# Softmax maxima of ordinary heads brought into the queries' row by two small DMAs instead of two identity matmuls and a PSUM copy

## What is computed

```python
s = jnp.einsum('bqhd,bkhd->bhqk', qb, kb).astype(jnp.float32) * scale + bias[None]
s = jnp.where(valid[None, None, None, :], s, MASK_VALUE)
p = jax.nn.softmax(s, axis=-1)
return jnp.einsum('bhqk,bkhd->bqhd', p.astype(vb.dtype), vb)
```

## Time and profile before

| what | value |
|---|---|
| median of 3 runs | 1634.67 us (1633.82 to 1635.09) |
| profiled execution, its own time | 1639.75 us |
| its span, first to last instruction | 1638.0 us |
| TensorE matmuls busy | 1580.3 us, 96% |
| VectorE, ScalarE, GpSimd busy | 1037.9, 826.2, 662.9 us |
| mean granted clock of TensorE | 0.988 |

### The profile page before, as it was taken

One profiled execution on the slowest core, in us unless ns is written; L12 is line 12 of the kernel. 1 busy time (PEld: TensorE's weight loads), 2 busy tenths in 40 slices (PEclk: granted clock), 3 DMA queues, 4 the chain that ended last, 5 costly groups with the idle time before them and its releaser, 6 DMA issues.

```text
span 1638.0 us, 42689 instructions
## 1 busy us (share of the span) xinstructions
PE 1580.3 (96%) x17344; PEld 1181.3 (72%) x17344; DVE 1037.9 (63%) x2134; ACT 826.2 (50%) x1541; POOL 662.9 (40%) x667
## 2 busy tenths in 40 slices
PE   7999999999999999999988999999999999999976
PEld 3455455458677777767767888899888899888853
DVE  7977867747565576556435666666666666666654
ACT  6655545522121111111125777767777777677763
POOL 2543433311101121111313655655655665656653
PEclk9999999999999999999998999999999999999978
DMA  6656566473524524542777877877777877778663
GB/s 245 218 193 219 188 212 221 181 258 147 207 75 169 206 96 150 181 167 79 222 220 185 208 196 199 198 187 192 171 193 196 201 192 184 172 190 197 158 170 84
DMA packets 306459, 299.99 MB, mean 183 GB/s; under 512 B 179384, under 2 KB 239816, under 8 KB 304216
## 3 DMA queue, kind: packets, MB, share of 16 engines
q1 hardware_dynamic: 305736, 296.60, 61.8%
q0 software_dynamic: 528, 0.66, 0.2%
HBM read 150.87 MB, written 83.54 MB: 143 GB/s over the span
## 4 chain that ended last, share of the span: by engine, by line
PE 68%; DMA 4%; POOL 2%; ACT 2%; SPq 2%; DVE 1%; issue 1%; DVEq 0%; ACTq 0%; POOLq 0%
PE bank L1154 10%; PE bank L2007 8%; PE bank L1130 6%; PE bank L1133 6%; PE bank L1132 6%; PE bank L1740 5%; PE bank L1742 5%; PE bank L1743 5%; DMA stages<-rows 4%; PE bank L1930 3%; PE bank L2061 2%; PE bank L2063 2%; PE bank L2062 2%; PE bank L2027 2%; PE bank L1933 2%
## 5 line engine op out<-in xcount | busy, mean ns | idle before, releaser
L1740 PE MATMUL bank<-middle,weights 128*128 128x128 f16 x1792 | 311.2, 220 | 2.3 <-ACT middle L1756 1.3
L1742 PE MATMUL bank<-middle,weights 128*128 128x128 f16 x1792 | 310.9, 220 | 0.0
L1743 PE MATMUL bank<-middle,weights 128*128 128x128 f16 x1792 | 310.8, 220 | 0.0
L2383 POOL TENSOR_TENSOR rows<-rows 128x640 f16<-128x640 f32 (+4 forms) x128 | 172.8, 1350 | 274.6 <-ACT rows L2184 274.6
L1130 PE MATMUL bank<-middle 128*128 128x256 f16 x784 | 213.7, 273 | 0.5 <-DVE stages L1270 0.5
L1133 PE MATMUL bank<-middle 128*128 128x256 f16 x784 | 213.7, 273 | 0.0
L1132 PE MATMUL bank<-middle 128*128 128x256 f16 x784 | 213.7, 273 | 0.0
L2007 PE MATMUL bank<-entry,stages 128*128 128x512 f16 x768 | 190.6, 386 | 5.3 <-DVE stages L2250 5.3
L1740 PEld LDWEIGHTS bank<-middle,weights 128*128 128x128 f16 x1792 | 176.0, 98 | 3.7 <-issue 2.8
L1742 PEld LDWEIGHTS bank<-middle,weights 128*128 128x128 f16 x1792 | 176.0, 98 | 0.4
L1743 PEld LDWEIGHTS bank<-middle,weights 128*128 128x128 f16 x1792 | 175.8, 98 | 0.0
(11 more groups left out here) (169 smaller groups left out, 3956.0 us busy)
## 6 DMA issues: line engine op xcount, KB each, us to landing
entry<-in_x SPq DMA_DIRECT2D x64, 512.0 KB, 3.8
h_ops<-middle SPq DMA_DIRECT2D x16, 1792.0 KB, 6.1
middle<-h_ops SPq DMA_DIRECT2D x112, 256.0 KB, 5.4
middle<-h_ops SPq DMA_DIRECT2D x49, 512.0 KB, 8.0
residual<-entry SPq DMA_DIRECT2D x32, 512.0 KB, 3.0
middle<-middle SPq DMA_DIRECT2D x128, 128.0 KB, 3.2
out<-entry SPq DMA_DIRECT2D x31, 512.0 KB, 2.9
entry<-residual SPq DMA_DIRECT2D x30, 512.0 KB, 5.6
```

Of the source, the lines that this page charges most:

```text
L1740: nc.tensor.matmul(dst, wh, hop3[:, o, 0, kt, :], start=(kt == 0 and s < 2 and pair == 0), stop=False, skip_group_check=True)
L1742: nc.tensor.matmul(dst, wh, hop3[:, o, 1, kt, :], start=False, stop=False, skip_group_check=True)
L1743: mm = nc.tensor.matmul(dst, wl, hop3[:, o, 0, kt, :], start=False, stop=(kt == 3), skip_group_check=True)
L2383: nc.gpsimd.tensor_tensor(r16[:, j, 1, c:640], r32[:, j, c:640], r16[:, j, 0, c:640], ALU.subtract).then_inc(A["rpl_done"], 1)
```

## The change

The identity matmuls, their semaphore `mrow_mm` and the copy from PSUM are gone. ScalarE, in the same place of its order, waits for the maxima and issues two DMAs from its own queue, each of which copies one float16 from each of 128 partitions of `m16` into 128 neighbouring places of partition 64 of `qm`. Each adds 16 to `mrow_done`, so what waited for a row now waits for 32. A wait for the scores of the same head in the tile before is added, since these read the row that is written over. The branch transposes no longer wait for rows; they wait for the bank's last reader in every round.

```diff
-        def max_rows(pe, t, h):
-            pe.wait_ge(A["max_done"], 2 * (HEADS * t + h + 1))
-            if t > 0 or h > 0:
-                pe.wait_ge(A["mrow_done"], HALF * t + h // 2)
-            for back in (h - 3, h - 2):
-                if back >= 0 and round_at(t, back):
-                    of, r = round_at(t, back)
-                    pe.wait_ge(A["ytl_done"], 2 * of + r + 1)
-            for j in range(2):
-                mm = nc.tensor.matmul(tra[:, j * P:(j + 1) * P], m16[:, h // 2 % 2, j:j + 1].to_broadcast([P, P]),
-                                      ident16[:, :], start=True, stop=True)
-            mm.then_inc(A["mrow_mm"], 1)
...
             if j == 0:
-                at_least(dve, A["mrow_mm"], HALF * t + h // 2 - 1)
+                at_least(dve, A["mrow_done"], 32 * (HALF * t + h // 2 - 1))
...
         def first_maxima(pe, x):
-            if x == 2:
-                max_rows(pe, 0, 0)
...
                 if k == 0:
-                    pe.wait_ge(A["mrow_done"], HALF * t + h // 2 + 1)
+                    pe.wait_ge(A["mrow_done"], 32 * (HALF * t + h // 2 + 1))
...
-            def branch_transposes(t, r, rows):
+            def branch_transposes(t, r):
...
-                pe.wait_ge(A["mrow_done"], rows)
-                if t == LAST and r > 0:
-                    pe.wait_ge(A["ytl_done"], 2 * t + r)
+                at_least(pe, A["ytl_done"], 2 * t + r)
...
-                    if t1 < ATILES:
-                        max_rows(pe, t1, h1)
...
             def max_row(t, h):
...
-                act.wait_ge(A["mrow_mm"], HALF * t + h // 2 + 1)
-                nc.scalar.activation(queries(qm, slice(DH, DH + 1), h, slice(0, AT)), tra[DH:DH + 1, 0:AT],
-                                     ACT.Copy).then_inc(A["mrow_done"], 1)
+                act.wait_ge(A["max_done"], 2 * (HEADS * t + h + 1))
+                if t > 0:
+                    act.wait_ge(A["st_mm"], seq(t - 1, h, len(groups(t - 1))))
+                for j in range(2):
+                    row = queries(qm, slice(DH, DH + 1), h, slice(j * P, (j + 1) * P))
+                    nc.scalar.dma_start(row, m16[:, h // 2 % 2, j:j + 1]).then_inc(A["mrow_done"], 16)
```

More of the change, by code:

```diff
@@ L1563, in build @@
             bias_k_loaded mask_done fg_loaded wob_hi wob_lo out_mm out_done
-            rows_set shift_done rexp_done rph_done rpl_done max_mm max_done mrow_mm mrow_done st_mm bias_done exp_done ph_done pl_done
+            rows_set shift_done rexp_done rph_done rpl_done max_mm max_done mrow_done st_mm bias_done exp_done ph_done pl_done
             pv_mm rc_done ya_done yt_mm yth_done ytl_done ss_done ms_done rstd_done fin_done""".split()
@@ L2090, in last_head @@
                 values(LAST, HEADS - 2)
-                branch_transposes(LAST, 1, HALF * ATILES)
+                branch_transposes(LAST, 1)
                 values(LAST, HEADS - 1)
@@ L2094, in last_head @@
                     output(LAST, i, 6, 9)
-                branch_transposes(LAST, 2, HALF * ATILES)
+                branch_transposes(LAST, 2)
                 for i in range(2, 4):
@@ L2126, in head @@
                     of, r = round_at(t, h)
-                    branch_transposes(of, r, min(HALF * t + (h + 1) // 2 + 1, HALF * ATILES))
+                    branch_transposes(of, r)
                 other(t, h, 2)
```

## The result

The changed kernel takes 1743.18 us (median of 4 runs, 1738.38 to 1748.16) against 1634.88 us before (4 runs); the ratio is 1.0663 with a 95% interval of 1.063 to 1.0697. It is 6.6% slower, 108 us. The profiled execution has a span of 1746.4 us against 1638.0.

A forecast was written before the change was run, and what follows sets the result against it. TensorE was taken to bound the attention part, 890 to 1550 us. Terms -6.1 - 0.2 + 1.0 = -5.3 us took 1634.67 to 1629.4 us, 0.32% faster; range 1626.5 to 1647 us, the forecast's own 1627 to 1632.

The forecast's parts named there:

- The bound: Attention part, 890 to 1550 us: TensorE busy 657.2 of 660 us, so only less TensorE work gains time.
- the rooms for L: Time from ScalarE's possible issue to the row's need, four places per tile: 4.16, 6.27, 4.45 and 4.49 us.
- the third place: Third ordinary head of a tile: 4.45 us from ScalarE's possible issue until the first score matmul needs the row.
- the 1.26 us: ScalarE's two DMA issues per row: 0.60 us each with 0.06 between, claimed to cost nothing.
- (c): ScalarE is held longer by its DMA issues, deciding from about 1.3 us per issue; 1650 us; chance 0.06.
- TensorE's 6 us: Saturated attention stretch: removing the identity matmuls of 55 rows at 0.11 us takes 6.1 us off the path.
- With one issue ahead, L is 0.06 + 0.66 + 2.6 = 3.3 us: Time from ScalarE's possible issue to the second DMA's landing, priced by 64 KB copies; no wait in tiles 2 to 14.
- my upper bound of 6.2: Longest expected time from ScalarE's possible issue to landing: 0.06 + 0.66 + 5.5 us, from a copy behind other traffic.
- Rival (a): Row lands late for the score matmuls, deciding from 4.5 us; 1658 us at 5.0, 1707 at 6.2; chance 0.22.
- the early rows: Two rows at the attention part's start with room of 2.98 and 2.56 us; TensorE stands 1.0 us together.
- Rival (b): Small DMAs stretch the transposing DMAs from 5.0 to 6.17 us, delaying ScalarE and GpSimd; 1651 us; chance 0.07.
- 256 pieces are few beside their own traffic: Argument that the row's pieces per pair would not slow transposing DMAs, which land in 5.0 us at 0.77 load.

The follow-up runs named there:

- the version with blocks: The changed kernel, with VectorE first transposing the maxima in 32 x 32 blocks, so each row DMA carries 4 pieces of 64 bytes; 1631.06 us, repeated 1632.49 us.
- the idle kernel: The kernel before, plus the change's two column-to-row DMAs per ordinary head into a spare row that no score waits for; 1718.61 us against 1634.33.

## Why the prediction was wrong

**What was right.** The bound: TensorE was saturated, and the rooms for L were the right thing to compute, though in the third place ScalarE issues as soon as the maximum is there and does not wait for its activation, so that room was 0.4 us longer than I had it (in the trace before, the maximum is there at 1246.19, and I counted from 1246.61). ScalarE's two issues took more than the 1.26 us that I had counted (1.87 us in the place shown and in the median), which is 0.9 us each, under the 1.3 us where (c) decides: behind them ScalarE stood for the next row maximum (L2160 waited 72.4 us for L1957 from 1000 to 1500 us). Of TensorE's 6 us the version with blocks gains 3.3 and 2.3 us by the medians. The rest is about the noise of such a comparison, and its cause is not shown; the transposes took 5.4 us in that kernel in place of 5.0.

**The step that failed** is "With one issue ahead, L is 0.06 + 0.66 + 2.6 = 3.3 us", with the price of a 64 KB copy for a DMA of 128 pieces of 2 bytes. The small DMAs of 1000 to 1500 us took 6.3 us each in the median, so L was about 0.5 + 6.3 = 6.8 us, as the pairs of the trace have it too, outside my upper bound of 6.2. (The 5.5 in that bound is of L1870, a copy of 128 KB and not of 64.) The sentence "for which no row has a price" named the hole, and I then filled it with the row nearest in size. The row was nearest in bytes and not in what counts: the issues of the 64 KB copies have 64 pieces of 1 KB, and they go to 64 partitions. With 4 pieces of 64 bytes L was 3.7 us, near the 3.3 of the sum: the term that was mis-sized is the price of the pieces.

**Rival (a)** is what happened to the scores, with L = 6.8: TensorE's matmuls waited 93 us for L2011 in a kernel that is 108 us longer. The lower clock adds at most 26 us and 6 us are saved, so these terms give 87 to 113 us. The formula of (a) gives at this L 2.64 + 0.53 + 2.35 + 2.31 = 7.8 us per tile, 102 us in 13 tiles, and with 8 for the early rows 1738 us. The waits measured are 93 / 16 = 5.8 us per tile, and the sum had no term for the clock, so it is in part luck that 1738 lies so near to 1743. I had put 0.22 on it, and its price at 6.2, 1707 us, lay outside my range.

**Rival (b)** happened as well: transposes at 8.3 us, where I had costed 6.2. "256 pieces are few beside their own traffic" misled: as packets they are few (0.6% of the engines), as completions they are not. Alone, with no score waiting, it is worth 84 us. The two don't add: 84 for (b) alone, 108 for both, and 31 us between the two kernels if TensorE's 7 us are counted; a TensorE that stands for a row gives ScalarE and GpSimd the time that they lost to the transposes. This is argued; the sign for it is that TensorE's weight loads waited 49.7 us for GpSimd in the idle kernel and 11.9 us in the changed one. Of the 31 us up to 23 can be the clock (mean 0.974, against 0.987 in the idle kernel).

**What the small writes do** is shown in size but not in mechanism. Shown: with 2-byte pieces it counts whether they go to one partition or to 128 (84 against 9 us with as many packets); 16 pieces of 16 bytes for the same bytes in one partition cost 5 us; neighbouring 2-byte places cost more than places 8 bytes apart (84 against 36 us); some 10 ns of delay of the transposes per write; and the other DMAs are held up, SyncE's copies too (2.6 to 3.9 us). That each such write reads, changes and writes back a few bytes and that these wait for each other would fit it. A rival that no run separates is that several DMA engines take turns at the one partition, whatever they write; the spread writes (36 us) speak against it as the whole, not as a part. No run here shows the mechanism directly. The Trainium skill (DMA: Bandwidth & Descriptors, Specifications) states that transfers below 512 bytes are done by read-modify-write. It makes no difference there between partitions, and the runs do: the column into 128 partitions has the same 2-byte pieces and costs 0.45%. The Trainium skill's rule (DMA: Bandwidth & Descriptors, Rules for kernel authors) that a strided last dimension becomes one descriptor per element, which I had weighed, agrees with the packets of this trace: 18432 = 128 DMAs x (128 + 16).

What stays open: why a DMA from ScalarE has its first packet 1.1 us later beside transposing DMAs, why few pieces stretch these from 5.0 to 5.4 us (5.6 from SyncE's own queue), and whether the number of writes or their size below some value is what costs.

## What to carry to other kernels

Cost a DMA by its pieces and by where they are written, before its bytes: 256 writes of 2 bytes into one partition delayed the landing of the other kinds of DMA by 1 to 3 us in the median, and their own packets (9 ns) show nothing of it. Where a column must become a row, cut the pieces first with a block transpose on an engine that has time; 8 pieces of 64 bytes did for 0.2% gained what 256 of 2 bytes did for 6.6% lost. And where the price of an added operation stands in no row, don't fill it with a row that has only the size in common; let the range reach over the rivals that hang on that price.

## What was unexpected of the hardware

Writing one partition in 2-byte pieces (84 us) costs about five times as much as reading one in such pieces (16 us), and nine times as much as writing to 128 partitions (9 us). The harm falls on others: with the idle DMAs, transposes of 5.0 us took 7.9. An issue from ScalarE held its sequencer for 0.48 us at best, 0.12 less than SyncE's 0.60 for copies of 64 KB (the second of a pair held it 1.37 us in the median), and it began while ScalarE's activation was still running (1250.72 against an end at 1251.69). And a late row can cost TensorE twice: after a wait of 2.88 us the granted clock was at 0.59 from 1258 to 1262 us.
